# HGRN scans of a hybrid SSM/attention step on one Trainium2 core: both directions of a token tile in one product

## What is computed

```
S_t = f_t * S_(t-1) + k_t v_t^T        o_t = q_t S_t
```

```python
att = einsum('bthd,btshd->bths', qc, decay * kc[:, None])      # decay = exp of summed log f between s and t
o = einsum('bths,bshv->bthv', att, vc) + einsum('bthd,bhdv->bthv', qc * exp(bcum), S)
S_new = exp(blast)[..., None] * S + einsum('bshd,bshv->bhdv', kc * exp(blast[:, None] - bcum), vc)
```

## Time and profile before

| | |
|---|---|
| median of 3 runs | 2413.52 us (2412.96 to 2415.86) |
| span of the profiled execution, the one that the rows are from | 2414.1 us, mean granted clock of PE 0.978 |
| busy in that span | PE 94%, its weight loads 83%, DVE 60%, ACT 35%, POOL 7% |
| first scan, `hgrn(0)`, on PE | 512.9 to 628.8 us |
| second scan, `hgrn(1)`, on PE | 765.1 to 880.9 us |

### The profile page before, as it was taken

One profiled execution on the slowest core, in us unless ns is written; L12 is line 12 of the kernel. 1 busy time (PEld: TensorE's weight loads), 2 busy tenths in 40 slices (PEclk: granted clock), 3 DMA queues, 4 the chain that ended last, 5 costly groups with the idle time before them and its releaser, 6 DMA issues.

```text
span 2414.1 us, 35260 instructions
## 1 busy us (share of the span) xinstructions
PE 2272.4 (94%) x14621; PEld 2003.9 (83%) x14621; DVE 1437.9 (60%) x2170; ACT 839.3 (35%) x1605; POOL 177.0 (7%) x217
## 2 busy tenths in 40 slices
PE   5989889989999998999999999999998999999998
PEld 3868867889888897779999999797555899999997
DVE  4357482348433867676465565777676675655654
ACT  4355372221121126343132222543555442322222
POOL 0000000024101320120000000200000100000002
PEclk9989999999999999999999999999899999999999
DMA  7411205520252012122132222122000022222221
GB/s 293 170 39 49 88 1 194 194 96 2 83 220 91 10 62 81 62 95 88 53 104 72 79 70 79 51 79 62 5 1 1 27 88 62 95 72 69 88 70 44
DMA packets 43565, 192.54 MB, mean 80 GB/s; under 512 B 4976, under 2 KB 4976, under 8 KB 36624
## 3 DMA queue, kind: packets, MB, share of 16 engines
q1 hardware_dynamic: 41184, 177.05, 21.6%
q0 software_dynamic: 2224, 13.24, 1.5%
HBM read 182.67 MB, written 7.60 MB: 79 GB/s over the span
## 4 chain that ended last, share of the span: by engine, by line
PE 84%; DVE 9%; ACT 3%; issue 2%; DMA 1%; POOL 0%; SPq 0%; ACTq 0%; DVEq 0%
PE pg L885 30%; PE pg L924 17%; PE pg L675 17%; PE ps L830 5%; PE ps L1115 2%; PE pg L1095 2%; PE ps L649 2%; PE pg L1070 1%; PE ps L771 1%; DMA ybuf<-in_wada 1%; PE ps L1070 1%; PE ps L790 1%; PE ps L793 1%; PE ps L748 1%; DVE wlo L1592 1%
## 5 line engine op out<-in xcount | busy, mean ns | idle before, releaser
L885 PE MATMUL pg<-hh,xhi 128*128 128x320 f32 (+2 forms) x1008 | 314.7, 312 | 9.8 <-DVE hl L1706 9.8
L885 PE MATMUL pg<-hl,xhi 128*128 128x320 f32 (+2 forms) x1008 | 312.1, 310 | 0.0
L885 PE MATMUL pg<-hh,xlo 128*128 128x320 f32 (+2 forms) x1008 | 312.0, 310 | 0.0
L1592 DVE TENSOR_TENSOR wlo<-ring,whi 128x1024 fp32r<-128x1024 f32 x127 | 154.5, 1221 | 189.9 <-ACT whi L1158 189.5
L675 PE MATMUL pg<-hh,whi 128*128 128x320 f32 x976 | 239.9, 328 | 22.9 <-DVE hl L1624 9.7
L675 PE MATMUL pg<-hl,whi 128*128 128x320 f32 x976 | 226.0, 313 | 0.0
L675 PE MATMUL pg<-hh,wlo 128*128 128x320 f32 x976 | 225.8, 313 | 0.0
L675 PEld LDWEIGHTS pg<-hh,whi 128*128 128x128 f32 x976 | 166.1, 192 | 61.6 <-issue 50.8
L885 PEld LDWEIGHTS pg<-hh,xhi 128*128 128x128 f32 x1008 | 192.3, 191 | 12.5 <-issue 12.4
L885 PE MATMUL pg<-hh,whi 128*128 128x320 f32 (+1 forms) x640 | 197.7, 309 | 0.0
L885 PE MATMUL pg<-hh,wlo 128*128 128x320 f32 (+1 forms) x640 | 196.7, 307 | 0.0
(11 more groups left out here) (330 smaller groups left out, 4621.7 us busy)
## 6 DMA issues: line engine op xcount, KB each, us to landing
ring<-in_wstream SPq DMA_DIRECT2D x229, 512.0 KB, 3.7
adaring<-in_wada SPq DMA_DIRECT2D x21, 1024.0 KB, 4.9
ybuf<-in_wada SPq DMA_DIRECT2D x21, 1024.0 KB, 5.0
adabig<-in_wada SPq DMA_DIRECT2D x6, 1024.0 KB, 19.1
xk<-in_x SPq DMA_DIRECT2D x1, 2560.0 KB, 11.4
yssd_scratch<-ybuf POOLq DMA_DIRECT2D x2, 1280.0 KB, 5.8
xk<-yssd_scratch POOLq DMA_DIRECT2D x1, 2560.0 KB, 10.3
xk<-in_x_tok POOLq DMA_DIRECT2D x1, 2560.0 KB, 9.2
```

Source lines behind the costliest of these rows:

```text
L885: last = nc.tensor.matmul(out, w[:, k * P:(k + 1) * P], h[:, k, a:b], start=k == 0 and m == 0, stop=k == KT - 1 and m == 2)
L1592: V.tensor_tensor(lo, flat(ring[:, s % RING]), hi.bitcast(F32), ALU.subtract).then_inc(wlo_ready, 1)
```

## The change

The five pairs become three waves: tiles 0 and 3, tiles 1 and 2, and the prompt tile. A tile has both directions at once. The two directions of a level use complementary halves of keys and of queries, so ACT merges the halves of `kg` of the two directions into one key block `km`, and the product's moving operand takes alternate runs of w queries from the two directions' rows of `hgq`. One product for each head and level then gives the blocks of both directions.

```diff
-HG_PAIRS = [(PROMPT_TT, PROMPT_TT), (0, 3), (1, 2), (2, 1), (3, 0)]
+HG_WAVES = ((0, 3), (1, 2), (PROMPT_TT,))
+HG_ROW = {0: 0, 3: 2, 1: 4, 2: 6, PROMPT_TT: 1}
+HG_MASKED = 5
...
+        def both_queries(h, tt, w):
+            return view(hgq[:], (HG_ROW[tt] * HG_SET + h) * P, [[2 * w, 64 // w], [HG_SET * P + w, 2], [1, w]])
...
+                if n == 4 * KT:
+                    sp.wait_ge(kk_ready[0], 3 * LEVELS)
                 sp.dma_start(ada_slot(n), wada[n]).then_inc(ada_loaded[n % ADA_RING], 16)
```

On PE, with `turn_keys`, `values`, `carried`, `chunk_state` for the four products or transposes of one tile and direction:

```diff
+                def level(p, e, i):
+                    u, tt = hg_units(e, 3 * g + p), HG_WAVES[p][e]
+                    pe.wait_ge(km_ready[e], LEVELS * u + i + 1)
+                    if i == 0:
+                        pe.wait_ge(q_started[e], u + 1)
+                    else:
+                        pe.wait_ge(qp_ready[e], hg_queries(e, 3 * g + p) + i)
+                    if i >= 2:
+                        pe.wait_ge(lv_masked[e], HG_MASKED * u + i - 1)
...
+                    heads(level_bank(p, e, i), lambda h: km[:, e, h, :], lambda h: both_queries(h, tt, 1 << i), lv_ready[e])
...
                 diagonals(0)
+                for i in range(LEVELS):
+                    for e in range(2):
+                        level(0, e, i)
+                    if i == 2:
+                        diagonals(1)
+                for i in range(LEVELS):
+                    for e in range(2):
+                        level(1, e, i)
+                    if i == 0:
+                        pe.wait_ge(kk_ready[0], LEVELS * (3 * g + 1))
+                        pe.wait_ge(dg_copied[0], 3 * g + 2)
+                        turn_keys(0, 0, w0)
...
+                        turn_keys(1, 3, w1)
+                    if i == 1:
+                        pe.wait_ge(kt_done, 8 * g + 1)
+                        pe.wait_ge(hst_in, 16 * (g + 1))
+                        pe.wait_ge(qp_ready[0], hg_queries(0, 3 * g + 1))
+                        values(0, 0)
+                        carried(0, 0, w0, o_ready)
...
+                    if i == 5:
+                        pe.wait_ge(hs_done, 6 * g + 1)
+                        diagonals(2)
+                for i in range(LEVELS):
+                    level(2, 0, i)
...
+                turn_keys(0, PROMPT_TT, ps[:, 2, :])
+                turn_keys(1, PROMPT_TT, ps[:, 0, :])
+                pe.wait_ge(o_copied, 5 * g + 4)
+                values(2, 0, o_ready, stop=True)
+                pe.wait_ge(hs_done, 6 * (g + 1))
+                carried(0, 3, o_bank[1], o_ready, start=True)
+                carried(1, 0, ps[:, 3, :], o_ready, start=True)
+                gemm(t_next)
+                pe.wait_ge(o_copied, 5 * (g + 1))
+                chunk_state(0, PROMPT_TT, ps[:, 1, :], 6)
+                pe.wait_ge(o_added, 2 * (g + 1))
+                chunk_state(1, PROMPT_TT, ps[:, 3, :], 7)
```

```diff
+                def merge(p, i):
+                    w = 1 << i
+                    for e, tt in enumerate(HG_WAVES[p]):
+                        n = LEVELS * hg_units(e, 3 * g + p) + i
+                        if n:
+                            act.wait_ge(lv_ready[e], n)
+                            act.wait_ge(kk_ready[e], n)
+                        for d in range(2):
+                            last = nc.scalar.copy(halves(km[:, e], w, d), halves(kg[:, d, :, tt * P:(tt + 1) * P], w, d))
+                        last.then_inc(km_ready[e], 1)
...
+                        for s in range(0, P, w):
+                            t = s ^ w
+                            last = nc.scalar.copy(att[s:s + w, e, p % 2, :, t:t + w],
+                                                  four(level_bank(p, e, i))[s:s + w, :, t:t + w])
...
+            def hgrn_end(g):
+                for d in range(2):
+                    act.wait_ge(hs_ready, 8 * g + 7 + d)
+                    nc.scalar.copy(hfin[:, d].rearrange("p h t -> p (h t)"), ps[:, 1 + 2 * d, :]).then_inc(hf_done, 1)
```

On DVE, for each level and tile: `queries` (one product over both directions' 512 elements; at level 0 two of 256), then `masked` below level 5. The decays and the start of the queries of the next wave stand between the levels of the wave before (first wave of a scan: between the last v tiles and `ada_bias`):

```diff
+                        if p < 2:
+                            if i == 2:
+                                hg_first_decays(g, p + 1)
+                            if i >= 3:
+                                hg_decays(g, p + 1, i - 2)
+                            if i >= 5 and i - 5 < len(HG_WAVES[p + 1]):
+                                hg_start(g, p + 1, i - 5)
+                        if p == 1 and i == 4:
+                            state(0, 0, w0, 0)
```

On POOL the key products are the same instructions, now both directions of a tile in a row, after the merge of that level; the transfer of `hfin` comes at the end of the scan:

```diff
-                            pool.wait_ge(lv_ready, n + 1)
+                            pool.wait_ge(km_ready[e], LEVELS * u + i + 1)
...
+                for d in range(2):
+                    pool.wait_ge(hf_done, 2 * g + d + 1)
+                    G.dma_start(hg_out[:, d, g * HG_SET:(g + 1) * HG_SET], hfin[:, d]).then_inc(hfin_out, 16)
             mixers_done(pool)
```

More of the change, by code:

```diff
@@ L488, in hybrid_step @@
         o_ready = sem("o_ready")
-        o_done = [sem(f"o_done{i}") for i in range(2)]
+        o_copied = sem("o_copied")
+        o_added = sem("o_added")
+        hf_done = sem("hf_done")
         hs_ready = sem("hs_ready")
@@ L1002, in _ @@
                 for i in range(16):
-                    gemm(t)
+                    if not (g and i == 0):
+                        gemm(t)
                     if i == 13 and g:
-                        pe.wait_ge(o_done[1], len(HG_PAIRS))
+                        pe.wait_ge(kt_done, 8)
+                        pe.wait_ge(hf_done, 2)
                     if i > 12:
@@ new lines, in hgrn @@
+                act.wait_ge(fk_ready, 8 * (g + 1))
+                if g:
+                    act.wait_ge(hfin_out, 32)
+                else:
+                    act.wait_ge(yssd_out, 32)
+                merge(0, 0)
+                opened(0)
+                decays(0)
+                for i in range(1, LEVELS):
+                    merge(0, i)
+                    if i == 3:
+                        opened(1)
+                blocks(0, 5)
+                merge(1, 0)
+                blocks(0, 6)
@@ new lines, in hgrn @@
+                decays(1)
+                for i in range(1, LEVELS):
+                    merge(1, i)
+                    if i == 1:
+                        keys_turned(0, w0)
+                        keys_turned(1, w1)
+                    if i == 2:
+                        out_copy(0, 0)
+                    if i == 3:
+                        out_copy(3, 1)
+                opened(2)
+                blocks(1, 5)
+                merge(2, 0)
+                blocks(1, 6)
+                decays(2)
@@ new lines, in hgrn @@
+                for i in range(1, LEVELS):
+                    merge(2, i)
+                    if i == 1:
+                        keys_turned(2, w0)
+                        keys_turned(3, w1)
+                    if i == 5:
+                        keys_turned(4, ps[:, 3, :])
+                        keys_turned(5, w0)
+                blocks(2, 5)
+                out_copy(1, 2)
+                out_copy(2, 3)
+                blocks(2, 6)
+                keys_turned(6, ps[:, 2, :])
+                keys_turned(7, ps[:, 0, :])
@@ L2323, in constant_arrays @@
     m8 = []
-    t = np.arange(P)
-    for d in range(2):
-        for i in range(LEVELS):
-            w = 1 << i
-            late = t.reshape(-1, 2, w)[:, 1 - d].reshape(-1)
-            same = (t[:, None] // (2 * w)) == (late[None, :] // (2 * w))
-            other = (t[:, None] // w) % 2 == d
-            m8.append(same & other)
-    m8.append(j == s)
+    for i in range(HG_MASKED):
+        w = 1 << i
+        m8.append((j // (2 * w) == s // (2 * w)) & (j // w != s // w))
     m8 = np.concatenate(m8, axis=1).astype(np.float32)
```

520 lines of the change are left out of this document (281 added, 239 removed).

## The result

| | before | after |
|---|---|---|
| median of 4 runs beside each other | 2414.4 us | 2347.5 us (2344.6 to 2349.7) |
| ratio | | 0.9721, interval 0.9709 to 0.9733 |
| profiled execution, span | 2414.1 | 2346.4 |

Predicted were 2351 us (2328 to 2388) and a faster kernel. The time is 3.5 us from the forecast, but part of that is luck: a gain of 6.35 us ahead of the scans, from two edits, was not in the sum, a loss of 2 came behind the scans, and inside a scan several terms were wrong in ways that made up the right total.

The account below looks back on a forecast made before the run. PE was taken to bound the kernel, with POOL pacing levels of two-tile waves. A scan gains 115.9 - (71.8 + 6 + 1) - 1.8 = 35.3; 2414.1 - 70.6 + 7.4 = 2350.9, predicted 2351 us (2328 to 2388).

Parts of the forecast that it names:

- PE's work and the halving of level products: In a scan, level products fall from 280 to 140; PE's work falls 35.7 us to 62.6.
- The drawing: Hand-drawn schedule of a scan before the projection tile: diagonals 3.6, waves 21.4, 24.2 and 22.7; 71.8 us for 115.9.
- Levels there are paced by POOL: In the two-tile waves, POOL's 2.6 us a level exceeds PE's 2 x 0.89 and DVE's 2.4.
- the prediction's own mark: Sign of a wrong pace: POOL has idle time beyond a quarter in waves 0 and 1.
- DVE and POOL in each other's way: Inside the waves, DVE products with two SBUF inputs and POOL's slow each other: 6 us a scan, half of 11.8.
- the rival by that name: POOL and DVE exclude each other for whole instructions: 14 to 25 us a scan, 2367 to 2389 us; chance 0.20.
- starving: DVE waits through POOL's run of products each time, 2.0 us: slower than before, 2475 us; chance 0.05.
- the 1 for hops: In a scan, 1 us added for hops that the schedule put at 0.1 to 0.2.
- Strided operand at nothing: Moving operand alternating single values of two rows at level 0: taken as 0, at most 4.5 us a scan.
- The end of the second scan: Prompt's states behind gemm(t_next) delay the next gemm: loss 5.4 us, plus 2 for low clock, 7.4.
- Nothing gives it back: Behind the second scan, the og stage recovers none of the loss, as norms pass from ACT to DVE's 4.15 us reciprocal.
- This start doesn't move: PE starts the first scan at 512.9 us as before; DVE's decays fill its idle time behind the last wlo.

Follow-up runs that it names:

- starts_ahead: Kernel after, with DVE's starts of the second wave's queries made ahead of the scan: 2343.4 us, ratio 0.9702 to before.
- pool_half: Kernel after, without POOL's forward key products at levels 1 to 5 of the first two waves: 2345.9 us, ratio 0.9724 to before.
- decays_out: Kernel after, with DVE's products of decays for the second wave, but the last, left out of the first wave: 2344.2 us, ratio 0.9711.
- psum_operand: Kernel after, with the second operand of DVE's decay and start products inside a scan read from PSUM, not SBUF: 2344.6 us, ratio 0.9720.
- plain_rows: Kernel after, with the moving operand of all level products as 128 values in a row: 2346.7 us, ratio 0.9729 to before.
- states_ahead: Kernel after, with the prompt's two state groups of the second scan ahead of the first og tile: 2341.8 us, ratio 0.9696 to before.
- both: Kernel after, with the edits of states_ahead and starts_ahead together: 2339.3 us, ratio 0.9692 to before.
- att_back: Kernel after, with DVE's memset of att and PE's wait for it put back, and masks at 512 KB: 2355.7 us, ratio 0.9751.

## Why the prediction came out

- **PE's work and the halving of level products: right.** 140 products a scan; groups are 0.89 apart from level 2 on.
- **The drawing, 3.6 + 21.4 + 24.2 + 22.7 = 71.8 (rounded).** Measured 5.3, 22.8, 28.1, 22.6 and 3.7, 22.8, 29.6, 23.3. The third wave is right. The first was drawn 1.4 too short, the second 3.9 and 5.4. The step that failed is the boundary, drawn as ACT's alone ("2.2 for blocks and the first merge of the next wave"): DVE's starts ended later still, and PE waited 1.98 us for them, worth 1.5, or 2.9 with the clock, by starts_ahead. Another 1.69 is the wait for ACT's merge at the head of the third wave, part of which is in the drawing's 3.6 of waits.
- **"Levels there are paced by POOL": wrong,** by the prediction's own mark: POOL idles for over a quarter of both waves, and pool_half moved the first by 0.56. Late in the first wave PE waited for DVE (decays_out), and at its end for ACT's merge.
- **DVE and POOL in each other's way, 6 us a scan: mis-sized.** Some 2.6 by psum_operand. The prediction took half of full exclusion. The rows show full exclusion, one instruction at a time: a DVE product that meets a running POOL product ends 0.28 us (256 elements) or 0.55 us (512) behind it, and a POOL product that meets DVE's waits in its turn. The Trainium skill ("SBUF — State Buffer", Who interferes with whom) has the second instruction fully blocked, and the trace agrees. The 0.52 of the earlier trace rows, which the prediction held against exclusion, is such a case too: POOL's first product ends at 519.40 and DVE's at 519.68. What was wrong is how much of it counts: DVE's waits come to 7.2 us in a scan, where 11.8 was put as the most that exclusion could cost, and some 2.6 of path hang on them. So the rival by that name had the right mechanism and, with 14 to 25 us, the wrong price; of starving there is none (in the thirteen traces no DVE product of queries, decays or starts took over 1.4 us). The 3.4 us too many, and the 1 for hops, stood in for about as much that the drawing had too short elsewhere: the first wave's 1.4, the clock on the diagonals (1.6) and some of the wait at the third wave's head. That the total of 78.8 came out to the tenth is luck.
- **Strided operand at nothing: wrong in price, right in effect.** It costs 0.45 us a group at level 0, half of the upper bound (4.5 us for five groups), and the first scan of plain_rows shows 0.3 us of it on the path; the second doesn't tell, since the clock differs. The Trainium skill (the same page, Door 1) would have level 0 alone pay; the trace agrees but for 0.07 a group at level 1.
- **The end of the second scan, 7.4: right in mechanism,** with the wait for `hfin` named. Measured 8.5 less 1.8 = 6.7. "Nothing gives it back" is not so: the seven `og` tiles behind are 1.5 shorter than before, and take 66.2 again when the states stand ahead (states_ahead, both).
- **"This start doesn't move": wrong.** It moved 6.35. The diff removed the memset and PE's wait for it, and made the transfer of masks 320 KB in place of 512, on the way to ACT's first activation; the sum has no term for either. att_back, with both put back, has 0.9 of its 6.33 at PE's first product, another 4.2 at the wait for the memset, and 1.3 by the lower clock behind it. The 0.9 can be the masks; no run has them alone.
- **What stands behind: 2 us slower** than in the trace of before, from 69.7 to 67.7, as the 1.5 of the `og` tiles less 3.5 in the stages after them. In the profiled runs of all thirteen kernels like after, PE took 1454 to 1457 us from its last `og` product to its last product, in the one trace of before 1452. Nothing there was edited. Whether one trace of before is low by chance stays open.

So the profiled span is 4.5 us below the sum of 2350.9: -6.35 at the start, -0.7 at the end of the second scan, +0.6 in the second scan itself (34.7 for 35.3), +2.0 behind the second `og` tile's start. The median is 1.1 above that span.

## What to carry to other kernels

Go through the removed lines of a diff for waits as carefully as through the added ones, also far from the code that it is about: a memset with a semaphore, 140 us ahead of the first scan, was most of the largest error here. Where several engines take nearly the same time for a step, price an edit by what stands next behind it; half of POOL's work was worth 0.56 us, while one pair of late DVE products at a wave's head was worth 1.5 to 2.9. A result that must be stored before buffers can be reused belongs ahead of the last large block of work, not behind it.

## What the runs showed of the hardware that I had not expected

- A float32 product whose moving operand alternates single values of two rows has its records 0.167 us apart in place of 0.111; with runs of two values 0.12; from four on there is no difference.
- DVE products with both inputs in SBUF and POOL's products took turns by whole instructions: two of DVE with 512 elements took 2.47 us beside POOL's and 1.28 with one input in PSUM, and POOL's four took 4.14 and 3.26. The one that was running first kept its time; the other ended a set distance behind it.
- The same stretch of PE's queue takes one of two lengths: the diagonals 3.68 or 5.3 us, the second wave 28.1 or 29.5, by the granted clock in it (for the diagonals 0.68 on average over the one window and 1.00 over the other, behind the same wait of 0.78 us). Over the 26 scans profiled here such steps of 0.6 to 1.6 us are most of what differs where the code is the same.
